# Memory scores: the products with the keys' rest over 64 rows, in the two halves of the array, with a bank per head

## The reference

```python
mk, mv = jnp.split(mem_n @ w_kv_mem[l], 2, axis=-1)
o_m = _cross_attention(m_q.reshape(bsz, seq, 4, 64), mk.reshape(bsz, 256, 4, 64), mv.reshape(bsz, 256, 4, 64))
# inside: s = einsum('bshd,bmhd->bhsm', q, k) * 64 ** -0.5; p = softmax(s); einsum('bhsm,bmhd->bshd', p, v)
y_m = (o_m * silu(m_gate)) @ p_m[l]
```

## Time and profile before

| | us |
|---|---|
| median of 3 runs | 1212.56 |
| lowest, highest | 1212.28, 1212.91 |
| the profiled execution | 1211.9 |
| its span | 1210.1 |
| TensorE busy | 1199.3 |
| VectorE, POOL, ScalarE busy | 790.7, 710.7, 544.6 |

### The profile page before, as it was taken

How to read it: one execution, slowest core, us unless ns; L and a number is a source line. 1 busy time by engine, 2 the same in 40 slices (tenths; PEclk the granted TensorE clock), 3 DMA queues, 4 the chain that set the end, 5 groups by cost and what they waited for, 6 DMA issues and landing times.

```text
span 1210.1 us, 15914 instructions
## 1 busy us (share of the span) xinstructions
PE 1199.3 (99%) x5772; PEld 1003.7 (83%) x5772; DVE 790.7 (65%) x1288; ACT 544.6 (45%) x997; POOL 710.7 (59%) x555
## 2 busy tenths in 40 slices
PE   9999999999999999999999999999999999999997
PEld 7888888888888888888888888888888888888886
DVE  5623865677576674428897666666667686877855
ACT  5433424344443444547474565656556444315000
POOL 6777887887777777878446445455533225558000
PEclk9999999999999999999999999999999999999999
DMA  8012131242323323233512111111002533377231
GB/s 280 15 55 70 35 105 35 70 140 101 108 105 105 131 92 126 105 106 118 196 48 60 36 53 53 36 53 52 20 18 101 187 115 113 105 250 253 79 123 69
DMA packets 91277, 118.61 MB, mean 98 GB/s; under 512 B 6072, under 2 KB 72632, under 8 KB 91200
## 3 DMA queue, kind: packets, MB, share of 16 engines
q1 hardware_dynamic: 90912, 117.34, 29.4%
q10 hardware_dynamic: 288, 0.26, 0.1%
HBM read 92.39 MB, written 25.20 MB: 97 GB/s over the span
## 4 chain that ended last, share of the span: by engine, by line
PE 91%; DVE 5%; ACT 2%; issue 1%; POOL 1%; DVEq 0%; ACTq 0%
PE pj L770 11%; PE pj L772 11%; PE pj L771 11%; PE pj L846 5%; PE pj L847 5%; PE pj L848 5%; PE pj L1119 4%; PE pt L770 3%; PE pt L772 3%; PE pt L771 3%; PE po L960 3%; PE pj L863 2%; PE pj L864 2%; PE pj L865 2%; PE pt L1119 2%; PE po L1119 2%
## 5 line engine op out<-in xcount | busy, mean ns | idle before, releaser
L1634 POOL TENSOR_TENSOR ring_lo<-w_pair,ring_hi 128x512 fp32r<-128x512 f32 x168 | 232.8, 1388 | 109.8 <-ACT ring_hi L1177 109.7
L1687 POOL TENSOR_TENSOR w_lo<-w_raw,w_hi 128x128 fp32r<-128x128 f32 (+1 forms) x104 | 113.0, 1105 | 131.4 <-ACT w_hi L1267 129.3
L1177 ACT ACTIVATE ring_hi<-w_pair 128x512 fp32r<-128x512 f32 x168 | 105.1, 628 | 160.4 <-PE pj L772 108.6
L1856 DVE SCALAR_TENSOR_TENSOR po<-glu,cwa,po 128x512 f32<-128x512 f32 x232 | 159.4, 747 | 20.6 <-ACT po L1228 20.6
L770 PE MATMUL pj<-t_hi,ring_hi 128*128 128x512 f32 x392 | 152.9, 390 | 0.3 <-DVE slot L1820 0.3
L771 PE MATMUL pj<-t_lo,ring_hi 128*128 128x512 f32 x392 | 152.5, 389 | 0.0
L772 PE MATMUL pj<-t_hi,ring_lo 128*128 128x512 f32 x392 | 152.5, 389 | 0.0
L846 PE MATMUL pj<-xT_hi,w_hi 128*128 128x512 f32 x320 | 126.2, 395 | 0.0
L847 PE MATMUL pj<-xT_lo,w_hi 128*128 128x512 f32 x320 | 125.3, 392 | 0.0
L848 PE MATMUL pj<-xT_hi,w_lo 128*128 128x512 f32 x320 | 125.2, 391 | 0.0
L1735 POOL TENSOR_SCALAR probs<-probs,rinv 128x128 f32<-128x128 f32 (+3 forms) x32 | 57.9, 1811 | 108.1 <-DVE rinv L2178 108.1
(11 more groups left out here) (394 smaller groups left out, 3001.9 us busy)
## 6 DMA issues: line engine op xcount, KB each, us to landing
w_pair<-in_w_in SPq DMA_DIRECT2D x28, 1024.0 KB, 5.2
gate_scratch<-slot SPq DMA_DIRECT2D x16, 1024.0 KB, 4.0
gate<-gate_scratch SPq DMA_DIRECT2D x32, 512.0 KB, 3.7
w_raw<-in_w_in SPq DMA_DIRECT2D x20, 512.0 KB, 3.9
z_scratch<-slot SPq DMA_DIRECT2D x8, 512.0 KB, 2.9
bias<-cum_scratch SPq DMA_DIRECT2D x8, 512.0 KB, 3.7
wout_raw<-in_w_out SPq DMA_DIRECT2D x8, 512.0 KB, 6.2
x_tok<-in_x SPq DMA_DIRECT2D x8, 512.0 KB, 4.3
```

What stands on the lines that cost most here:

```text
L1177: nc.scalar.activation(ring_hi[:, j % RING, :, :], w_src(u, p), ACT.Copy).then_inc(s_rhi, 1)
L1634: nc.gpsimd.tensor_tensor(ring_lo[:, j % RING, :, :], w_src(u, p), ring_hi[:, j % RING, :, :], ALU.subtract).then_inc(s_rlo, 1)
L1687: nc.gpsimd.tensor_tensor(w_lo[:, j % 2, k, :], w_raw[:, j % 2, k, :], w_hi[:, j % 2, k, :], ALU.subtract).then_inc(s_wlo, 1)
L1856: nc.vector.scalar_tensor_tensor(out=acc if n < PAD_A else src, in0=src, scalar=cwa[:, ct, n:n + 1], in1=acc, op0=ALU.mult, op1=ALU.add).t ...
```

## The change

mscores writes head 0 into bank 2 and head 1 into bank 3; a unit uses one half of both banks, by w % 2. The two products with km_hi stay as they are. The two with km_lo are over 64 rows each, rows 0 to 63 for head 0 and 64 to 127 for head 1, so that q_lo k_lo is no longer added. km_lo is made only in the half that is read. As two units share the banks, mscores(w) waits for the exponentials of unit w - 1, from w = 1 on. mscores(1) is moved behind the last weigh of branch C.

```diff
+        def memory_scores(w):
+            return pj[:, 2:4, w % 2 * MEM:(w % 2 + 1) * MEM]
...
-                if w >= 2:
-                    pe.wait_ge(s_e, UN + w - 1)
+                if w:
+                    pe.wait_ge(s_e, UN + w)
+                q = (q_stack, q_stack1)[m][:, :, i * P:(i + 1) * P]
                 for a in range(2):
-                    q = (q_stack, q_stack1)[m][:, a, i * P:(i + 1) * P]
-                    o = pj[:, 2 + w % 2, a * MEM:(a + 1) * MEM]
-                    nc.tensor.matmul(o, q, km_hi[:, 2 * m + a, :], start=True, stop=False)
-                    mm = nc.tensor.matmul(o, q, km_lo[:, 2 * m + a, :], start=False, stop=True)
+                    nc.tensor.matmul(memory_scores(w)[:, a, :], q[:, a, :], km_hi[:, 2 * m + a, :],
+                                     start=True, stop=False)
+                for a in range(2):
+                    rows = slice(DH * a, DH * a + DH)
+                    mm = nc.tensor.matmul(memory_scores(w)[:, a, :], q[rows, a, :], km_lo[rows, 2 * m + a, :],
+                                          start=False, stop=True)
                 mm.then_inc(s_s, 1)
...
             mscores(0)
+            weigh(CT - 1, UNITS // 2 - 1)
             mscores(1)
-            weigh(CT - 1, UNITS // 2 - 1)
...
                     op = nc.scalar.activation(probs[:, w % 2, a * MEM:(a + 1) * MEM],
-                                              pj[:, 2 + w % 2, a * MEM:(a + 1) * MEM], ACT.Exp,
+                                              memory_scores(w)[:, a, :], ACT.Exp,
...
             def km_lo_part(c, a):
-                b, o = DH * a, DH * (1 - a)
+                b = DH * a
                 dve.wait_ge(s_kvh, 2 * c + a + 1)
-                for r in (b, o):
-                    op = nc.vector.tensor_tensor(km_lo[r:r + DH, 2 * c + a, :], po[b:b + DH, c, 0:MEM],
-                                                 km_hi[b:b + DH, 2 * c + a, :], ALU.subtract)
-                op.then_inc(s_kvl, 1)
+                nc.vector.tensor_tensor(km_lo[b:b + DH, 2 * c + a, :], po[b:b + DH, c, 0:MEM],
+                                        km_hi[b:b + DH, 2 * c + a, :], ALU.subtract).then_inc(s_kvl, 1)
...
             def mmax(w):
                 dve.wait_ge(s_s, UN + w + 1)
-                nc.vector.tensor_reduce(rmin[:, w % 2, :], pj[:, 2 + w % 2, :].rearrange("p (a k) -> p a k", a=2),
-                                        AX.X, ALU.max).then_inc(s_dm, 1)
+                nc.vector.tensor_reduce(rmin[:, w % 2, :], memory_scores(w), AX.X, ALU.max).then_inc(s_dm, 1)
```

## The result

The changed kernel takes 1217.01 us (median of 6 runs, 1216.38 to 1217.67) against 1212.43 us of the kernel before in 6 runs (1212.07 to 1212.91). The ratio is 1.0037, 95% interval 1.0024 to 1.0050: 4.6 us slower, where 1213.0 us was forecast and the range ended at 1216.0. Rival (a) came nearest: each change of the number of rows costs TensorE time, 0.28 us a unit in all, where I had reckoned 0.43. That the array runs empty at such a change, the reason that I gave for it, fits the traces but is not shown by them.

A forecast was written before the change was run, and what follows sets the result against it. TensorE's row was taken to bound the kernel. Start +0.96 and nine units -0.54 gave +0.42 us on 1211.9, so 1212.3, and with 0.66 to the median 1213.0; range 1211.6 to 1216.0.

The forecast's parts named there:

- Rival (a): Memory attention units: array runs empty at each change of rows, 0.27 us per change, 1218.6 us in total; chance 0.22.
- What bounds the kernel: Whole kernel: TensorE, busy 1199.3 of 1210.1 us, sets the time; a change counts only where TensorE isn't waiting.
- The products: Score products of a unit: two of four go to 64 rows, may run side by side; saving 0 to 0.117 us, 0.06 taken.
- g: Saving per unit of scores from the 64-row pair: 0.117 us side by side, 0 one after the other, 0.06 taken.
- the nine units that I counted: Units 2 to 7 and 11 to 13, whose saving was to count: nine x 0.06 = -0.54 us.
- The order at the start: Start of memory attention: scores(1), now behind the weigh, waits for unit 0's exponentials; loss 1.02 - g, +0.96 us.
- The new wait in the other units: Units after the start: scores(w) waits for exponentials of unit w-1, always met in time; least slack 1.37 us.
- rival (c): Each unit: the later release costs the weight prefetch, 14 x 0.11 = 1.5 us, +1.0 on the forecast, 1214.0; chance 0.07.
- What of the saving counts: Fourteen units: savings in 8 to 10, 14, 15 are lost at holds; delays free there up to 0.97 and 0.45 us.
- The keys' rest: Making km_lo, 628 to 635 us: four instructions instead of eight save VectorE about 1.7 us, worth nothing to the total.
- Rival (b): 64-row pair in each unit: runs one after the other, held by its loads; +1.02 us, 1213.6; chance 0.20.
- Rival (d): All units: all the saving counts and the start costs nothing; 16 x 0.117 = 1.9 us, 1210.7; chance 0.03.

The follow-up runs named there:

- the first experiment: Changed kernel with the products of the keys' rest over 128 rows again: 1213.39 us against 1212.69 of the kernel before, ratio 1.0005.

## Why the prediction was wrong, step by step

**What bounds the kernel:** right. TensorE's row sets the time, and the account above closes from that row alone.

**The products: the step that failed.** "If one after the other, 0.234 and g = 0", with a middle of 0.06 taken and everything below nothing left to a rival. I priced the pair and not the way into it and out of it. Side by side came true in full (0.12 for the pair, the upper end of g); but two changes of rows, a term that the sum put at nothing and left to rival (a), cost 2 x 0.197 = 0.39 us a unit. Together a unit costs 0.27 more by its price, and 0.28 in the account above, instead of 0.06 less. Over the start and the nine units that I counted this is 10 x 0.34 = 3.4 us, nearly all of the miss from 1213.0 to 1217.0.

Half of the evidence was in the row that I used: a load in the open costs 0.11. I asked only whether the pair's second load would be hidden, and not whether the first, and the one of the fill product behind, can be loaded ahead across a change of rows. They are not: 0.10 to 0.11 of each c is the load, and some 0.09 comes before it. The load behind a change begins 0.07 us before the product in front of it ends, in both directions: the second 128-row product of unit 2 goes from 937.24 to 937.52 and the pair's load begins at 937.45, the pair ends at 937.84 and the fill product's load begins at 937.77. (Ends of products are modelled in the trace.) That fits an array that runs empty with the load laid over the last part of it, where I had added the two (0.16 + 0.11). No run here takes them apart, so what c is made of stays open.

The Trainium skill (TensorEngine Tiling (Array Packing), "Key Properties") says that a change of tiling mode drains TensorE. The traces agree in that every change costs, 0.197 us each; the emptying itself they don't show. I had the rule in the text and gave its rival a chance of 0.22. The Trainium skill's other statement (TensorE: Matmul & The Clock Gate, "Part 3: Packing small matmuls"), that products in different row groups start within about 4 ns of each other, holds here too: the records of a pair are 3 to 4 ns apart in all sixteen units. Both held together; in the sum I had let one of them in and not the other.

**The order at the start:** right in mechanism and size. 1.02 - g gives 1.29 to 1.30 with the g of -0.27 to -0.28 that the other units show, and 1.30 was measured; with 128-row products (g = 0) 1.02 was seen; with the waits filled it goes. ScalarE's end of the exponentials did not move (928.70, or 929.58 - 0.87 = 928.71).

**The new wait in the other units:** right. TensorE's list has one wait for the exponentials, the one at the start, and rival (c) falls with the first experiment.

**What of the saving counts:** right in kind, too generous for a loss. Of a loss, 0.27 and 0.45 us were free instead of 0.97 and 0.45, because the chain to zb_lo waits for TensorE once more on its way and its own steps got longer. With the true size of a unit, the nine and the free amounts would have given 1.30 + 9 x 0.28 + 0.11 = 3.9 us, where the trace has 4.3.

**The keys' rest:** right, nothing. The offset of 0.82 at 50 us is 0.86 at 603 and 0.87 at 870: nothing moved TensorE by more than 0.01 us between 628 us, where the rest is made, and 870. The maximum over two banks takes 0.687 us on the mean, 0.685 before.

**Rival (b)** falls: the pair is side by side. **Rival (d)** falls: the kernel got slower, and the start cost its 1.02 us. **Rival (a)** had the step that failed right, a cost at each change of rows, with 0.27 a change where 0.197 was measured.

## What to carry to other kernels

Splitting a product into halves of the array pays only over a stretch: here two changes of rows cost 0.39 us and each pair of 256-column products saved 0.117. So by an estimate from these two numbers it loses below four pairs between two changes, and four pairs would gain 0.08 us; no kernel with its pairs gathered was run. Before a change of an instruction's form is priced by the instruction, price its neighbours: what was loaded ahead for them may now lie in the open. And an instruction that stands in front of a wait is free only there: moving scores(1) behind it cost 1.02 us, its own 0.47 and 0.55 for a wait and an open load of its own, until other work was moved into the gaps.

## What was not expected of the hardware

The change between 128-row and 64-row products costs 0.195 to 0.20 us on the average of there and back, in three kernels with two, four and two changes a unit. A 64-row product alone costs as much as a 128-row one of the same columns: a second one in the same half added 0.12 us, one in the other half added nothing. The two of a pair always wrote to different banks here, so a pair into one bank stays untested.
